# GLA level products as 32- and 64-column blocks in column tiles, three levels in one copy, and moved schedule tables

## What is computed

```
inter = einsum(qc * exp(b), s)                        # b: running sum of the log decays in the chunk
attn  = einsum('bihk,bjhk,bijhk->bhij', qc, kc, exp(b_i - b_j))   # for j <= i
o     = inter + attn @ v                              # once forward, once on the flipped sequence
```

## Time and profile before

| what | value |
|---|---|
| median of 3 runs | 1441.1 us (1439.16 to 1444.92) |
| the profiled execution, and its span | 1441.68 us, 1439.8 us |
| mean granted TensorE clock | 0.992 |
| PE busy, weight loads beside it | 97%, 91% of the span |
| DVE, ACT, POOL busy | 62%, 42%, 39% |

### The profile page before, as it was taken

How to read it: one execution, slowest core, us unless ns; L and a number is a source line. 1 busy time by engine, 2 the same in 40 slices (tenths; PEclk the granted TensorE clock), 3 DMA queues, 4 the chain that set the end, 5 groups by cost and what they waited for, 6 DMA issues and landing times.

```text
span 1439.8 us, 21521 instructions
## 1 busy us (share of the span) xinstructions
PE 1395.1 (97%) x8555; PEld 1315.1 (91%) x8555; DVE 896.4 (62%) x1122; ACT 603.9 (42%) x832; POOL 565.6 (39%) x237
## 2 busy tenths in 40 slices
PE   6999999999999999999999999999999999999998
PEld 3887998999998999999979889899999899999998
DVE  4559977995764488666565899698858432111022
ACT  3553434545734333332236344345464443333231
POOL 1353544444463100000025444444436545555552
PEclk9999999999999999999999999999999999999998
DMA  9865232433542766557424323243336434343441
GB/s 334 290 207 173 85 102 89 118 103 97 181 161 89 245 229 216 188 176 245 154 84 143 95 89 103 80 131 91 102 115 207 138 98 137 126 132 120 130 131 60
DMA packets 159212, 208.60 MB, mean 145 GB/s; under 512 B 9228, under 2 KB 126984, under 8 KB 159112
## 3 DMA queue, kind: packets, MB, share of 16 engines
q1 hardware_dynamic: 158560, 207.00, 44.9%
q10 hardware_dynamic: 552, 0.22, 0.1%
HBM read 204.05 MB, written 3.15 MB: 144 GB/s over the span
## 4 chain that ended last, share of the span: by engine, by line
PE 74%; DVE 11%; ACT 5%; DMA 4%; issue 2%; POOL 2%; SPq 1%; DVEq 0%; ACTq 0%; POOLq 0%
PE ps L834 22%; PE ps L836 21%; PE ps L835 21%; POOL w_lo L703 2%; DMA w_raw<-in_w_in_dram 1%; DVE conv_acc L1803 1%; ACT w_hi L1356 1%; DVE fac L1937 1%; DVE attn L1947 1%; DMA w_raw<-in_w_out_dram 1%; PE ps L1087 1%; PE ps L881 1%; DVE gates L2099 1%; DVE t L1762 1%; PE ps L882 1%
## 5 line engine op out<-in xcount | busy, mean ns | idle before, releaser
L703 POOL TENSOR_TENSOR w_lo<-w_raw,w_hi 128x1024 fp32r<-128x1024 f32 (+1 forms) x229 | 562.1, 2456 | 850.6 <-ACT w_hi L1356 728.5
L834 PE MATMUL ps<-h_hi,w_hi 128*128 128x384 f32 x1600 | 546.5, 342 | 6.5 <-DVE h_lo L1768 3.8
L836 PE MATMUL ps<-h_hi,w_lo 128*128 128x384 f32 x1600 | 535.7, 335 | 0.0
L835 PE MATMUL ps<-h_lo,w_hi 128*128 128x384 f32 x1600 | 535.6, 335 | 0.0
L1356 ACT ACTIVATE w_hi<-w_raw 128x1024 fp32r<-128x1024 f32 x199 | 207.6, 1044 | 434.2 <-PE ps L836 303.7
L834 PEld LDWEIGHTS ps<-h_hi,w_hi 128*128 128x128 f32 x1600 | 300.7, 188 | 21.7 <-issue 10.0
L835 PEld LDWEIGHTS ps<-h_lo,w_hi 128*128 128x128 f32 x1600 | 300.9, 188 | 1.4
L836 PEld LDWEIGHTS ps<-h_hi,w_lo 128*128 128x128 f32 x1600 | 300.8, 188 | 0.0
L1803 DVE SCALAR_TENSOR_TENSOR conv_acc<-conv_in,cw,conv_acc 128x399 f32<-128x399 f32 x240 | 210.7, 940 | 1.8
L1659 ACT ACTIVATE w_hi<-w_raw 128x1024 fp32r<-128x1024 f32 x88 | 93.2, 1061 | 211.4 <-PE ps L836 151.8
L834 PE MATMUL ps<-act_hi,w_hi 128*128 128x384 f32 x352 | 118.4, 336 | 0.0
(11 more groups left out here) (262 smaller groups left out, 1656.4 us busy)
## 6 DMA issues: line engine op xcount, KB each, us to landing
w_raw<-in_w_in_dram SPq DMA_DIRECT2D x112, 512.0 KB, 3.6
w_raw<-in_w_ffn_in_dram SPq DMA_DIRECT2D x88, 512.0 KB, 3.5
mod_late<-in_w_mod_dram SPq DMA_DIRECT2D x71, 512.0 KB, 5.3
w_raw<-in_w_ffn_out_dram SPq DMA_DIRECT2D x44, 512.0 KB, 3.7
w_raw<-in_w_branch_dram SPq DMA_DIRECT2D x24, 512.0 KB, 3.4
mod_early<-in_w_mod_dram SPq DMA_DIRECT2D x16, 512.0 KB, 6.6
w_raw<-in_w_out_dram SPq DMA_DIRECT2D x16, 512.0 KB, 3.4
mod_second<-in_w_mod_dram SPq DMA_DIRECT2D x9, 512.0 KB, 11.1
```

The source lines that it names most:

```text
L703: nc.gpsimd.tensor_tensor(m["w_lo"][:, n % SPL, cols], m["w_raw"][:, n % RAW, cols], m["w_hi"][:, n % SPL, cols].bitcast(F32), ALU.subtrac ...
L834: mm(out, hi[:, at:at + P], rhs[0][:, k, :], start=start, stop=False)
L835: mm(out, hi[:, at:at + P], rhs[1][:, k, :], start=False, stop=False)
L836: ins = mm(out, lo[:, at:at + P], rhs[0][:, k, :], start=False, stop=stop)
```

## The change

`level` forms each product in blocks: 32 columns of keys against 32 of queries, at the partitions of PSUM that belong to those keys, so that each block lies in one column tile. Levels -1 to 4 need the four blocks on the diagonal, level 5 the four beside it (`q = b ^ 32`), level 6 two blocks of 64 (`q = b ^ 64`). Nothing else of the square is written. Levels 4, 5 and 6 write different parts of the same banks, so they are copied together, once, after level 6, under one mask; levels 5 and 6 wait on PE for the level before and for the copy of level 3 only. The number of `copied` signals and the places that wait for them follow. The masks of levels 5 and 6 are added to that of level 4 at the start. Tables move.

```
 LEVELS = 7
+WIDE = 4
@@ level, PE
-                        pe.wait_ge(*copied.at(l, 3 * (i + 1)))
+                        pe.wait_ge(*copied.at(l, 3 * (min(i, WIDE) + 1)))
+                        if i > WIDE:
+                            pe.wait_ge(*level_done.at(l, i + 1))
...
-                        if i < 0:
-                            return mm(out, part("gqk", 1, hh, tt), part("gqk", 0, hh, tt), start=True, stop=True)
-                        f = f"fac{i % 2}"
-                        return mm(out, part(f, 1, hh, tt), part(f, 0, hh, tt), start=True, stop=True)
+                        keys, queries = (part("gqk" if i < 0 else f"fac{i % 2}", side, hh, tt) for side in (1, 0))
+                        n = 64 if i == LEVELS - 1 else 32
+                        for b in range(0, P, n):
+                            q = b ^ n if i > WIDE else b
+                            ins = mm(out[b:b + n, q:q + n], keys[:, b:b + n], queries[:, q:q + n], start=True, stop=True)
+                        return ins
@@ masks, DVE
-                    v.tensor_copy(m["masks"][:], m["masks_in"][:]).then_inc(masks_v.sem, 1)
+                    wide = m["masks_in"][:, WIDE, :]
+                    for i in range(WIDE + 1, LEVELS):
+                        v.tensor_tensor(wide, wide, m["masks_in"][:, i, :], ALU.add).then_inc(masks_v.sem, 1)
+                        dve.wait_ge(masks_v.sem, i - WIDE)
+                    v.tensor_copy(m["masks"][:], m["masks_in"][:, 0:WIDE + 1, :]).then_inc(masks_v.sem, 1)
@@ build and copy_level, DVE
-                        dve.wait_ge(*copied.at(l, 3 * (i - 1)))
+                        dve.wait_ge(*copied.at(l, 3 * min(i - 1, WIDE + 1)))
...
+                    if WIDE <= i < LEVELS - 1:
+                        return
...
-                        mask = m["masks"][:, i:i + 1, :].unsqueeze(1).broadcast_to([P, 2, 2, P])
+                        mask = m["masks"][:, min(i, WIDE):min(i, WIDE) + 1, :].unsqueeze(1).broadcast_to([P, 2, 2, P])
@@ tables
-LEVEL_AT_0 = [10, 12, 14, 16, 17, 20, 21, 23, 26]
+LEVEL_AT_0 = [10, 12, 13, 15, 17, 20, 21, 23, 26]
-GATE_AT = [5, 6, 6, 6, 6, 7, 8, 8]
-EARLY_LOAD = [7, 8, 8, 9, 9, 14, 15, 15, 16, 16, 16, 18, 18, 21, 21, 22]
-EARLY_AT = [11, 11, 11, 11, 11, 12, 12, 13, 16, 16, 16, 16, 17, 17, 18, 18]
+GATE_AT = [6, 6, 6, 6, 6, 7, 8, 8]
+EARLY_LOAD = [7, 8, 8, 9, 9, 14, 15, 16, 16, 16, 16, 18, 18, 21, 21, 22]
+EARLY_AT = [11, 11, 11, 11, 11, 12, 13, 13, 16, 16, 16, 16, 17, 17, 17, 18]
-PUT_ACT_0 = [14, 19, 24]
-CACHE_KEYS_AT_0 = 23
+PUT_ACT_0 = [14, 20, 24]
+CACHE_KEYS_AT_0 = 22
-LEVEL_TAPS_0 = [0, 2, 8, 7, 4, 7, 7]
-WEIGHT_TAPS_0 = [2, 5, 3, 0, 6, 3, 2, 5, 6, 2, 6, 8]
+LEVEL_TAPS_0 = [0, 4, 8, 7, 4, 7, 7]
+WEIGHT_TAPS_0 = [0, 5, 3, 0, 6, 3, 2, 5, 6, 2, 6, 8]
-SELF_AT_1 = 6
-TURN_AT_1 = [11]
-TAKE_ACT_1 = [11]
+SELF_AT_1 = 8
+TURN_AT_1 = [12]
+TAKE_ACT_1 = [10]
-LEVEL_TAPS_1 = [1, 2, 6, 7, 1, 7, 10]
-MAX_TAPS_1 = [1, 2, 2, 1, 2, 3, 1, 4, 0, 4, 6, 1]
-WEIGHT_TAPS_1 = [2, 5, 3, 0, 6, 3, 2, 5, 6, 2, 6, 8]
+LEVEL_TAPS_1 = [1, 2, 6, 7, 1, 7, 9]
+MAX_TAPS_1 = [1, 2, 4, 1, 3, 3, 1, 4, 1, 4, 6, 1]
+WEIGHT_TAPS_1 = [2, 5, 2, 0, 6, 3, 2, 5, 6, 2, 6, 8]
```

More of the change, by code:

```diff
@@ L122 @@
 STATE_ACT_0 = 39
-GLA_HI_ACT_0 = 42
+GLA_HI_ACT_0 = 41
 SCORE_ACT_0 = [38, 39, 41, 43, 44, 46, 48, 49, 51, 53, 55, 57, 59, 61]
-LEVEL_TAPS_0 = [0, 2, 8, 7, 4, 7, 7]
+LEVEL_TAPS_0 = [0, 4, 8, 7, 4, 7, 7]
 STATE_TAPS_0 = 15
@@ L185 @@
 STATE_ACT_1 = 39
-GLA_HI_ACT_1 = 42
-SCORE_AT_1 = [34, 35, 37, 39, 40, 42, 44, 45, 47, 48, 51, 53, 55, 57]
+GLA_HI_ACT_1 = 41
+SCORE_AT_1 = [34, 35, 37, 39, 40, 42, 44, 45, 47, 48, 51, 53, 55, 56]
 SCORE_ACT_1 = [38, 39, 41, 43, 44, 46, 48, 49, 51, 53, 55, 57, 59, 61]
-LEVEL_TAPS_1 = [1, 2, 6, 7, 1, 7, 10]
+LEVEL_TAPS_1 = [1, 2, 6, 7, 1, 7, 9]
 STATE_TAPS_1 = 16
 OUT_TAPS_1 = [5, 6, 6, 1]
-MAX_TAPS_1 = [1, 2, 2, 1, 2, 3, 1, 4, 0, 4, 6, 1]
-WEIGHT_TAPS_1 = [2, 5, 3, 0, 6, 3, 2, 5, 6, 2, 6, 8]
+MAX_TAPS_1 = [1, 2, 4, 1, 3, 3, 1, 4, 1, 4, 6, 1]
+WEIGHT_TAPS_1 = [2, 5, 2, 0, 6, 3, 2, 5, 6, 2, 6, 8]
 HEAD_SUM_AT_1 = [41, 46, 52]
@@ L329, in memory @@
     own("ones", [P, P])
-    own("masks", [P, LEVELS, P], U8)
+    own("masks", [P, WIDE + 1, P], U8)
     own("wa", [2 * RANK, 2, 256])
@@ L447, in program @@
         even_heads = signal("even_heads", ROUNDS + 1)
-        copied = signal("copied", 3 * (LEVELS + 1) + 2)
+        copied = signal("copied", 3 * (WIDE + 2) + 2)
         entered = signal("entered", 4)
@@ L962, in whole @@
                     pe.wait_ge(*factors.at(l, i + 1))
-                    pe.wait_ge(*copied.at(l, 3 * (LEVELS + 1)))
+                    pe.wait_ge(*copied.at(l, 3 * (WIDE + 2)))
                     for hh in (0, 2, 1, 3):
@@ L994, in gla_out @@
                     if hh == 0:
-                        pe.wait_ge(*copied.at(l, 3 * (LEVELS + 1) + 2))
+                        pe.wait_ge(*copied.at(l, 3 * (WIDE + 2) + 2))
                         pe.wait_ge(*entered.at(l, 4))
@@ L1467, in exp_scores @@
                     if u == 0:
-                        act.wait_ge(*copied.at(l, 3 * (LEVELS + 1) + 2))
+                        act.wait_ge(*copied.at(l, 3 * (WIDE + 2) + 2))
                         act.wait_ge(*etot_a.at(l, 2))
```

## The result

| | before | after |
|---|---|---|
| median | 1443.3 us | 1445.2 us |
| range | 1439.2 to 1451.4, 20 runs | 1442.0 to 1452.0, 20 runs |
| ratio, 95% interval | | 1.0022 [1.0012, 1.0033] |
| profiled span | 1439.8 us | 1442.9 us |

The account below looks back on a forecast made before the run. PE was taken as the bound (open 97% of the span). Layer 0's gain of 7.1 and layer 1's of 4.7 make 11.8 us, off the median 1441.1: 1429.3, told as 1429.5, range 1419 to 1444.

Parts of the forecast that it names:

- The products: Level matmuls on PE: 96 block records a level, started 7 ns apart, take 0.80 us in place of 1.54.
- rival of 1.5 or 2.75 us: Time per level if blocks overlap only two at a time (1440.5, chance 0.09) or each record costs a fixed price (1460, 0.11).
- At most 7.5 ns apart: Starts of matmuls in different column tiles, read from four `mod_mm` matmuls followed 0.03 us later by four more.
- Sixteen levels x (1.54 - 0.80) = 11.8 us less PE work: PE's saving over the levels of both layers, 5.9 us in each, before changes in waits.
- some 20: Sign of a wrong forecast: PE's waits in the GLA stretch exceeding some 20 us, against 13.7 before.
- the chain keeps the clock: Rival: pieces, casts and DVE set the pace up to level 4, so PE only waits longer; 1436.7, chance 0.08.
- One `mod_mm` moves from piece 5 to 6, so the decay ... come 0.5 us earlier: Layer 0 start: decay and first exponential 0.5 us earlier, PE 0.74 earlier, so level 0's wait grows by 0.2.
- the put: Layer 0: vector 3's `mod_put` goes behind the cast of piece 20 and a `mod_mm` waits for it, +0.75 us (0 to 1.1).
- Level 2, now ahead of piece 14 ... waits about 3 there ... in place of the 3.1: Layer 0: PE waits for level 1's copy (0.8 to 4.7) instead of the convolution's input, -0.1 us.
- Two copies of 2.0 us go from DVE ... all but the 1.5 lies beside PE: Each layer: fewer mask copies save only level 6's 1.5 us wait in layer 0; up to 4 a layer if DVE were late.
- Half of that 1.0 is counted (-0.5): Layer 0, level 2: it lasted 2.51 us at half clock after a wait; removing this was counted as -0.5 us.
- Layer 1: the sum: Layer 1's waits: -0.6 at levels -1 and 0, +0.2 at level 2, +1.6 at level 4; +1.2, so it gains 4.7.

Follow-up runs that it names:

- e1: The kernel before with the block products alone; copies, masks and tables as before: 1439.9 us, ratio 0.9964.
- e10: The kernel before with convolution steps between the levels cut to 16 of 399 columns (output not the reference's): 1438.9 us, ratio 0.9976.
- e11: e1 with convolution steps between the levels cut to 16 of 399 columns (output not the reference's): 1433.2 us, ratio 0.9933.
- e16: Block products, merged copy and layer 1's new tables (1441.1 us without more), plus layer 0's new modulation tables: 1444.1 us, ratio 0.9998.
- e15: Block products, merged copy and layer 1's new tables (1441.1 us without more), plus layer 0's levels 2 and 3 a piece earlier: 1446.4 us, ratio 1.0002.
- e2: The changed kernel with every table as in the kernel before, so block products and merged copy only: 1439.3 us, ratio 0.9972.
- e7: e2 with nine convolution steps of each layer moved from between the levels to behind them: 1438.4 us, ratio 0.9965.
- e8: e1 with nine convolution steps of each layer moved from between the levels to behind them: 1443.2 us, ratio 0.9999.
- e4: The changed kernel with five convolution steps of each layer moved behind the merged copy: 1443.3 us, ratio 0.9996.
- e6: The kernel before, products and copies unchanged, with all tables of the changed kernel: 1444.0 us, ratio 1.0014.

## Why the prediction was wrong, point by point

- **The products: right in kind, the term too large.** 96 records a level, loads of 106 ns, no rival of 1.5 or 2.75 us. But 0.98 us a level (about 10 ns a start, not 7), so 0.56 saved and not 0.74: 9.0 and not 11.8 at full clock. "At most 7.5 ns apart" divides 0.03 us by four starts, which have three gaps: the rows allowed 10 ns, and 96 x 10 is 0.96, near what came. By the 25 ns from start to start of the Trainium skill (TensorE: Matmul & The Clock Gate, "Wait — 56ns, not 53.3ns?") a level would take 2.4 us, an estimate; the 0.98 decides against it for matmuls in different tiles.
- **"Sixteen levels x (1.54 - 0.80) = 11.8 us less PE work", all of it put on the path: the first step that failed.** e1 has 8.1 us less work, but wins 5.2. The waits were held fixed or moved by a microsecond; in truth a wait can be the end of a loop from PE over ACT and DVE back to PE, which takes a saving inside it. That is shown before level 4 of layer 1 (e10 to e11, +0.57 for 0.56 saved); for the other waits it is inferred. In the changed kernel's trace PE's waits in the GLA stretch came to 20.2 us, where 13.7 stood, just over the "some 20" that was told as a sign of being wrong. The rival "the chain keeps the clock", at 0.08, was nearest in kind: it set 1436.7, and e1, from the same 1441.1, stands at 1435.9. That it is levels 5 and 6 that still win, as it has it, no run shows.
- **"One `mod_mm` moves from piece 5 to 6, so the decay ... come 0.5 us earlier": failed.** The load that waits for that slot was not followed on SP. Stall of 2.4 and 0.7 us at pieces 10 and 9, and half clock at 85.4. With the put (1.06 us, where 0.75 stood) it is what e16 carries: some 2.6 us, not clear of the noise by itself.
- **"Level 2, now ahead of piece 14 ... waits about 3 there ... in place of the 3.1": too cheap.** The wait itself was 2.2 (0.8 to 4.7 was told), but by e15 the two levels moved together cost some 3 us, again not clear of the noise by itself.
- **"Two copies of 2.0 us go from DVE ... all but the 1.5 lies beside PE": failed.** With the steps where they are the two copies won nothing (e2 against e1; 4.9 us where nine steps are moved, e7 against e8), and the price of a late DVE was asked at level 6, not at `whole`, which waits for the same last copy: 3.2 and 3.0 us, of which e4 shows 3.8 us of time.
- **"Half of that 1.0 is counted (-0.5)" for the clock: failed in size and sign.** 30.7 us at half clock in place of 13.7. The 17 us more cost up to 8.5, most of the 11.8 that were to be won. The Trainium skill, same page, Part 1 ("The HAM clock gate"), puts the price of the ramp, told there for a kernel's start, below 1% of a typical span. Here the half clock came back behind waits all through the kernel, and the 30.7 us cost up to 15.4, 1.1% of the span, somewhat more.
- **Layer 1: the sum was near, the parts were not.** Level 2 waited 3.6 (2.9 was told) and level 4 2.6 (4.3), since DVE, which had no pause there in the kernel before, waits for the exponential in the changed one.

By the ratios, in us: products -5.2, merged copy +1.2, tables of layer 1 +1.2, levels 2 and 3 of layer 0 +3.2, modulation tables +2.6, the rest of layer 0's tables, of which no run has them alone, about 0: +3 in all. That sum is as measured by the way it is made, since each kernel stands on the one before it; only the split of layer 0's 6.1 is a check. Each of these terms is uncertain by 2 to 3 us, and hangs on the order: the tables cost 2 us in the kernel before (e6), the copy wins 4.9 with moved steps (e7, e8). How much of each wait's cost is the half clock behind it is not settled, and one trace of a kernel can stand over 4 us off its median (e7: 1434.2 profiled, 1438.4 median). The clock does differ from execution to execution: over the 350 that have it on record, an execution was some 0.9 us longer than another of the same kernel for each 0.001 that its mean granted clock was lower, which is 2.9 us more at half clock. The mean was 0.991 for the kernel before and 0.987 for the changed one, so some 4 us between them go along with the clock; what of that is the clock itself, and what the waits ahead of it, these runs do not part.

## What to carry to other kernels

When the bound engine gets less to do, ask of each of its waits where the chain that ends there began. If it began on the same engine, time saved inside that chain comes back at that wait; the gain is only what lies outside of such loops. When a use is moved to a later place, follow the buffer that it frees to the load that waits for it, and to everything that stands behind that load in its queue. A wait of 2 to 4 us on TensorE is to be priced with the half clock that may follow it, as it did behind six of seven here.

## What the runs showed of the hardware

- Matmuls of 32 columns in eight tiles start about 10 ns apart (96 records in 0.98 us), each open for 186 to 267 ns, 210 in the median; 48 of 64 columns take 0.90 us.
- In the changed kernel's trace six of the seven waits of 2.0 us or more behind the first 30 us were followed by half clock for 3.4 or 6.8 us; after the one before 836.97 (2.6 us) the clock stayed full, where in the kernel before a wait of 2.7 at the same place was followed by it.
- Some steps of DVE take very different times, others do not: seven convolution steps took 4.03, 6.17 and 8.06 us with POOL open for 0.7, 3.2 and 5.2 of them, while three predicated copies stayed at 1.93 to 2.00.
